# FFN of a four-layer decoder step: four plain tiles instead of three ahead of the paired ones, the input sums spread over two of them, the first down weights split ahead of the last gated value, adaLN loads spaced

## The reference

```
s1, a1, g1, s2, a2, g2 = split(silu(c) @ ada_w[i] + ada_b[i])
x <- LN(ALPHA * x + g1 * mixer(x * (1 + a1) + s1))
h  = x * (1 + a2) + s2
x <- LN(ALPHA * x + g2 * ((silu(h @ wg) * (h @ wu)) @ wd))      # wg, wu: 1024 x 2816, wd: 2816 x 1024
```

## Time and profile before

| | |
|---|---|
| median of 3 runs | 3110.5 us (3109.71 to 3116.89) |
| profiled execution | 3103.62 us, its span 3101.8 us |
| TensorE busy | 2932.5 us, 95% of the span |
| VectorE, ScalarE, GpSimd busy | 53%, 30%, 56% |
| mean granted TensorE clock | 0.98 of full speed |

### The profile page before, as it was taken

How to read it: one execution, slowest core, us unless ns; L and a number is a source line. 1 busy time by engine, 2 the same in 40 slices (tenths; PEclk the granted TensorE clock), 3 DMA queues, 4 the chain that set the end, 5 groups by cost and what they waited for, 6 DMA issues and landing times.

```text
span 3101.8 us, 53473 instructions
## 1 busy us (share of the span) xinstructions
PE 2932.5 (95%) x21172; PEld 2700.2 (87%) x21172; DVE 1653.5 (53%) x3161; ACT 934.4 (30%) x1825; POOL 1734.0 (56%) x1209
## 2 busy tenths in 40 slices
PE   6999989999999989999989998999999999899997
PEld 4799989999976879999986687999997999899997
DVE  3254684636554774635565547463553536846263
ACT  2220152414220442414234324241422211424141
POOL 2455456857666456767620154676764565468575
PEclk8999999999999999999999999999999999999999
DMA  6643333443345433444321433344422323222332
GB/s 239 224 116 86 119 114 98 136 130 102 99 122 159 151 120 97 162 126 160 94 64 56 115 122 104 109 151 130 157 74 83 102 85 93 62 82 82 87 92 72
DMA packets 450486, 354.85 MB, mean 114 GB/s; under 512 B 26120, under 2 KB 424832, under 8 KB 437933
## 3 DMA queue, kind: packets, MB, share of 16 engines
q1 hardware_dynamic: 435744, 324.79, 34.0%
q10 hardware_dynamic: 14493, 26.63, 2.9%
HBM read 337.86 MB, written 5.25 MB: 111 GB/s over the span
## 4 chain that ended last, share of the span: by engine, by line
PE 76%; DVE 10%; ACT 4%; DMA 2%; issue 2%; DVEq 2%; POOL 1%; ACTq 1%; POOLq 1%; SPq 1%
PE pb L1142 75%; DMA w_raw<-in_ffn_w_up 2%; DMA ada_first<-in_ada_w 1%; DVE part L2727 1%; ACT h_hi L2134 1%; ACT hf L2134 1%; DVE h_lo L2787 1%; DVE xa L2753 1%; DVE pb L2746 1%; DVE hf L2768 0%; DVE h_lo L2777 0%; PE pb L1978 0%; DVE a_lo L2594 0%; POOL a_lo L1048 0%; DVE part L2722 0%
## 5 line engine op out<-in xcount | busy, mean ns | idle before, releaser
L978 POOL TENSOR_SCALAR w_hi<-w_raw 128x1024 fp32r<-128x1024 f32 (+2 forms) x264 | 277.9, 1053 | 714.5 <-DMA w_raw<-in_gmlp_w_in 279.3
L981 POOL TENSOR_TENSOR w_lo<-w_raw,w_hi 128x1024 fp32r<-128x1024 f32 (+2 forms) x264 | 625.8, 2370 | 44.0 <-issue 44.0
L1142 PE MATMUL pb<-a_hi,w_hi 128*128 128x288 f32 x2176 | 601.7, 300 | 33.9 <-POOL w_hi L978 31.9
L1142 PE MATMUL pb<-a_lo,w_hi 128*128 128x288 f32 x2176 | 595.6, 297 | 0.0
L1142 PE MATMUL pb<-h_hi,w_hi 128*128 128x288 f32 x2064 | 548.7, 302 | 47.0 <-DVE pr L2939 19.4
L1142 PE MATMUL pb<-h_lo,w_hi 128*128 128x288 f32 x2064 | 528.7, 297 | 0.0
L1023 POOL TENSOR_TENSOR w_lo<-w_raw,w_hi 128x512 fp32r<-128x512 f32 x304 | 400.8, 1340 | 163.7 <-DVE s_raw L2979 106.6
L1142 PEld LDWEIGHTS pb<-a_hi,w_hi 128*128 128x128 f32 x2176 | 414.2, 190 | 42.1 <-issue 35.5
L1142 PEld LDWEIGHTS pb<-h_hi,w_hi 128*128 128x128 f32 x2064 | 382.8, 191 | 62.3 <-DVE pr L2939 20.4
L1142 PEld LDWEIGHTS pb<-a_lo,w_hi 128*128 128x128 f32 x2176 | 414.7, 191 | 0.7
L1142 PEld LDWEIGHTS pb<-h_lo,w_hi 128*128 128x128 f32 x2064 | 378.7, 191 | 0.0
(11 more groups left out here) (373 smaller groups left out, 4950.5 us busy)
## 6 DMA issues: line engine op xcount, KB each, us to landing
ada_w<-in_ada_w SPq DMA_DIRECT2D x80, 1024.0 KB, 8.9
w_raw<-in_ffn_w_gate SPq DMA_DIRECT2D x88, 512.0 KB, 3.9
w_raw<-in_ffn_w_up SPq DMA_DIRECT2D x88, 512.0 KB, 3.9
w_raw<-in_gmlp_w_in SPq DMA_DIRECT2D x64, 512.0 KB, 4.2
w_raw<-in_ffn_w_down SPq DMA_DIRECT2D x64, 512.0 KB, 5.0
w_raw<-in_gmlp_w_out SPq DMA_DIRECT2D x32, 512.0 KB, 4.9
w_raw<-in_ffn_w_down SPq DMA_DIRECT2D x32, 384.0 KB, 3.7
w_raw<-in_conv_w_pw SPq DMA_DIRECT2D x24, 512.0 KB, 4.2
```

What stands on the lines that cost most here:

```text
L978: nc.gpsimd.tensor_scalar(w_hi[:, s, 0:w], w_raw[:, s, 0:w], 1.0, 1.0, ALU.mult, ALU.mult).then_inc(split_hi, 1)
L981: nc.gpsimd.tensor_tensor(w_lo[:, s, 0:w], w_raw[:, s, 0:w], w_hi[:, s, 0:w].bitcast(F32), ALU.subtract).then_inc(split_lo, 1)
L1142: return nc.tensor.matmul(out, lhsT, rhs, start=start, stop=stop)
```

## The change

- Tile 3 of each layer becomes plain (`PAIRED_FROM = 4`), so four plain tiles run ahead of the first paired one, and two paired tiles are left in group 0.
- VectorE makes `t1`, then the two gated values of tiles 0 and 1, and only then `t3` and the changed `h`; the gated values of the plain tiles are formed in the bank of the up product (`gated_in_bank`): the product frees the gate's bank, and the `a_lo` subtraction the other. ScalarE's and GpSimd's orders follow: GpSimd makes `t4` ahead of the first pair's forms.
- At the end of a group the slots are taken in another order (`sums_end`): the slots of the tile before the last come first, then slot 4, then those of the last tile. GpSimd splits the first two down units ahead of the last tile's `gated_lower`.
- adaLN loads are asked for by `ada_asked`, one to four at a time, and two at a time ahead of the fifth and the seventh down unit of groups 0 and 1.

```diff
@@ -53,7 +53,8 @@
-PAIRED_FROM = 3
+GU = ((0, 6), (6, 8), (14, 8))
+PAIRED_FROM = 4
 QK = KT // 2
@@ -80,6 +81,18 @@
+def ada_asked(l, m):
+    if m <= 2:
+        return ADA1
+    done = [t for t in ada_groups(l)[0] if t <= m - 2]
+    if not done:
+        return ADA_FIRST + (0, 1, 2, 4)[min(m, 5) - 2]
+    last = max(done)
+    apart = any(last < first <= m for first, _ in GU)
+    return ada_used_by(l, m - 2) + (ADA1 if apart else min(ADA1, m - last))
@@ -523,7 +536,6 @@
-        GU = ((0, 6), (6, 8), (14, 8))
@@ -537,7 +549,8 @@
                 self.slot, self.prior, self.ordinal = [], [], []
-                self.held, self.last, self.whole = [None] * SLOTS, SLOTS - 1, 0
+                self.held, self.whole = [None] * SLOTS, 0
+                self.order, self.at, self.pairs = list(range(SLOTS)), 0, []
                 self.sums_free = {}
@@ -545,10 +558,12 @@
                 self.freed.append(None)
-                s = (self.last + 1) % SLOTS
-                if paired and s == SLOTS - 1:
-                    s = 0
-                self.last = s
+                if paired and self.order[self.at % SLOTS] == SLOTS - 1:
+                    self.at += 1
+                s = self.order[self.at % SLOTS]
+                self.at += 1
+                if paired:
+                    self.pairs = (self.pairs + [s])[-4:]
                 self.slot.append(s)
@@ -563,6 +578,7 @@
                 self.held[SLOTS - 1] = ("after", (acc_ready, self.products))
+                self.order, self.at = self.pairs[:2] + [SLOTS - 1] + self.pairs[2:], 0
@@ -692,7 +708,7 @@
                     plan.mark[l, "m", m] = len(plan.srcs)
-                    if m == 2:
+                    if m == PAIRED_FROM - 1:
                         plan.mark[l, "turned"] = plan.products - 2
@@ -859,8 +875,12 @@
                             load_to(plan.mark[l, "m", m])
-                            ada_to(l + 1, ADA1 if m < 4 else ada_used_by(l + 1, m - 3) + ADA1)
+                            ada_to(l + 1, ada_asked(l + 1, m))
                         if n < 2:
+                            load_to(plan.mark[l, "d", n] - 4)
+                            ada_to(l + 1, ada_used_by(l + 1, m) + 2)
+                            load_to(plan.mark[l, "d", n] - 2)
+                            ada_to(l + 1, ada_used_by(l + 1, m) + ADA1)
                             load_to(plan.mark[l, "d", n])
@@ -1067,14 +1087,13 @@
                         lower(t3_lo[:], t3_raw[:], t3_hi[:], t_low)
-                    forms_early(l, ms[0], FQ.n)
-                    if n == 0:
-                        pool.wait_ge(t_sum, 2 * l + 2)
+                        pool.wait_ge(t_sum, 3 * l + 3)
                         nc.gpsimd.tensor_tensor(t4_raw[:], h_hi[:, QK:, half_cols(0)].bitcast(F32), hf[:, 1],
                         pool.drain().then_inc(t4_made, 1)
+                    forms_early(l, ms[0], FQ.n)
                     for m in ms:
@@ -1083,8 +1102,9 @@
                             forms_early(l, m + 1, FQ.n)
+                    U.up(2 * len(ms))
+                    split_to(U.n + 2)
                     gated_lower(ms[-1] - GU[n][0])
-                    U.up(2 * len(ms))
@@ -1605,10 +1625,11 @@
                     first_halves(wait_h, 1, slots)
-                    s_a, s_b = take_units(2)
-                    for h in (1, 0):
-                        for s in (s_a, s_b):
-                            half_product(s, KT, h, (h_hi, h_lo))
+                    for _ in range(2, PAIRED_FROM):
+                        s_a, s_b = take_units(2)
+                        for h in (1, 0):
+                            for s in (s_a, s_b):
+                                half_product(s, KT, h, (h_hi, h_lo))
                 for m in paired_tiles(n):
@@ -2245,21 +2266,28 @@
                 if n == 0:
-                    for dst, src, at_ in ((t1_hi, t1_raw, 1), (t3_hi, t3_raw, 1)):
-                        act.wait_ge(t_sum, 2 * l + at_)
-                        fn(dst[:], src[:], ACT.Copy).then_inc(t_hi, 1)
                     first_gates()
-                    residuals(t, 0, 5)
+                    act.wait_ge(t_sum, 3 * l + 1)
+                    fn(t1_hi[:], t1_raw[:], ACT.Copy).then_inc(t_hi, 1)
+                    residuals(t, 0, 3)
+                    act.wait_ge(t_sum, 3 * l + 2)
+                    fn(t3_hi[:], t3_raw[:], ACT.Copy).then_inc(t_hi, 1)
                     gate(0, G.n % BANKS, ACT.Silu)
-                upper_gate(l, ms[0])
+                    residuals(t, 3, 6)
+                    gate(1, G.n % BANKS, ACT.Silu)
+                    upper_gate(l, ms[0])
+                    residuals(t, 6, 9)
+                    gate(0, G.n % BANKS, ACT.Silu)
+                    act.wait_ge(t_sum, 3 * l + 3)
+                    act.wait_ge(acc_ready, plan.mark[l, "turned"])
+                    fn(h_hi[:, 0:QK, half_cols(1)], hf[:, 1], ACT.Copy).then_inc(t_hi, 1)
+                else:
+                    upper_gate(l, ms[0])
                 upper_up(l, ms[0])
                 if n == 0:
-                    act.wait_ge(t_sum, 2 * l + 2)
-                    act.wait_ge(acc_ready, plan.mark[l, "turned"])
-                    fn(h_hi[:, 0:QK, half_cols(1)], hf[:, 1], ACT.Copy).then_inc(t_hi, 1)
+                    residuals(t, 9, 12)
                     gate(1, G.n % BANKS, ACT.Silu)
-                    residuals(t, 5, 10)
                 for m in ms:
@@ -2273,7 +2301,7 @@
                     if n == 0:
-                        residuals(t, 10 + 2 * (m - ms[0]), 11 + 2 * (m - ms[0]))
+                        residuals(t, 12 + 2 * (m - ms[0]), 13 + 2 * (m - ms[0]))
                     if m != ms[-1]:
@@ -2282,7 +2310,7 @@
                     if n == 0:
-                        residuals(t, 11 + 2 * (m - ms[0]), 12 + 2 * (m - ms[0]))
+                        residuals(t, 13 + 2 * (m - ms[0]), 14 + 2 * (m - ms[0]))
                     G.up(7)
@@ -2950,6 +2978,23 @@
+            def gated_in_bank(m, h, q):
+                up = pb[:, (G.n + 1) % BANKS, 0:HALF]
+                dve.wait_ge(acc_ready, G.n + 2)
+                dve.wait_ge(sg_ready, SG.up())
+                v.tensor_tensor(up, up, sg[:, q, :], ALU.mult).then_inc(acc_free, 1)
+                dve.drain()
+                v.tensor_copy(one(a_hi, m, half_cols(h)), up)
+                dve.drain()
+                v.tensor_tensor(one(a_lo, m, half_cols(h)), up, one(a_hi, m, half_cols(h)).bitcast(F32),
+                                ALU.subtract)
+                dve.drain().then_inc(a_ready, 1)
+                dve.sem_inc(acc_free, 1)
+                G.up(2)
@@ -3051,22 +3096,25 @@
                     v.tensor_tensor(t1_raw[:], t1_raw[:], h_lo[:, 0:QK, half_cols(0)].bitcast(F32), ALU.subtract)
+                    dve.drain().then_inc(t_sum, 1)
+                    for m in range(2):
+                        gated_in_bank(m, 1, m)
                     v.tensor_tensor(t3_raw[:], hf[:, 1], hf[:, 0], ALU.subtract)
                     ada_pairs(l + 1, ADA_FIRST * more)
-                    for m in range(2):
-                        gated(m, 1, m)
+                    gated_in_bank(2, 1, 0)
                     dve.wait_ge(t_hi, 4 * l + 1)
                     v.tensor_tensor(t1_lo[:], t1_raw[:], t1_hi[:].bitcast(F32), ALU.subtract).then_inc(t_lo_dve, 1)
+                    gated_in_bank(2, 0, 1)
                     form_sums(l, ms[0], FQ.n)
-                    gated(2, 1, 0)
+                    gated_in_bank(3, 1, 0)
                     dve.wait_ge(t_hi, 4 * l + 3)
                     form_lows(l, FQ.n)
-                    gated(2, 0, 1)
+                    gated_in_bank(3, 0, 1)
                 for m in ms:
```

## The result

The changed kernel takes 3022.4 us in the median (3020.06 to 3023.16, four runs) against 3110.5: 0.9711 of the time before, 95% interval 0.9694 to 0.9728, 88 us less. The forecast was 3025. The profiled execution takes 3020.06 us, its span 3018.3, which is 83.5 us less than before.

The account below looks back on a forecast made before the run. With TensorE at 95% of the span, gains come only where it idles or runs at its low clock. Starts 35.8, ends 41.7 and loads 7.8 sum to 85 us, from 3110.5 to 3025 us, range 3004 to 3070.

Parts of the forecast that it names:

- The starts: Four FFN starts: 41.0 us idle plus 16 of clock, less 14.8 of waits and 6.4 of added work, gains 35.8 us.
- left-over waits: TensorE's waits remaining at the FFN starts after the change: 3.7 us a layer, 14.8 in all.
- The three that the prediction names: Waits per start: first gated value 1.1 us, `w_lo` of tile 2's up 1.5, sum beside `t4_lo` 1.1.
- to 448.3: Layer 0's start: GpSimd's splits of tile 3's weights end at 448.3, wanted from 448.7; tile 3's 12.8 us cover later work.
- Rival 2: FFN starts gain nothing: GpSimd's two more splits make it last to be ready; 3067 us, chance 0.11.
- the clock: FFN starts: granted clock below 1 puts the windows 19 us short of full speed, of which 16 us taken as gain.
- The wait beside `t4_lo`: FFN starts: the sum for the next pair runs beside GpSimd's `t4_lo`; 0.7 to 1.5 us, taken as 1.1.
- The ends: Nine group ends, before the down products: 32.7 us idle plus 14 of clock, less 5 left over, gains 41.7 us.
- Rival 3: Ends gain nothing: a down unit lands late, GpSimd stands on it, TensorE waits in the second pass; 3067 us, chance 0.08.
- The loads: Inside the groups, adaLN loads delaying an up weight: 8.1 us idle plus 1.7 of clock, less 2 left, gains 7.8 us.
- rival 5: Slower: adaLN loads ahead of the fifth down unit make it land late, 120 us in all; 3145 us, chance 0.05.
- Rival 1: Short waits at the starts still drop the clock: 12 times 1.7, 20 us lost; 3045 us, chance 0.10.

Follow-up runs that it names:

- run 10: Changed kernel with the `w_hi` of tile 3's two weights cast by ScalarE in place of GpSimd: 3012.6 us, 0.9698.
- run 9: Changed kernel with four reorderings on VectorE, ScalarE and GpSimd, one for each wait left at the FFN starts: 3015.1 us, 0.9704.
- run 6: Changed kernel with `t3` and the fourth input sum again ahead of the first two gated values on VectorE, four plain tiles kept: 3024.2 us, 0.973.
- run 4: Changed kernel with the old slot rotation and the down weights' split behind the last `a_lo`, both end parts undone: 3069.5 us, 0.9879.
- Run 3: Changed kernel with the old rotation of slots at the group ends, the early split of the down weights kept: 3040.1 us, 0.9777.
- second trace: The changed kernel itself, measured again beside run 10 and 11: 3017.1 us, 0.9718.
- 11: The kernel of run 10 with three of the four reorderings of run 9, GpSimd's order as in the changed kernel: 3013.0 us, 0.9698.

## Why the prediction was right, and where its terms were not

**The starts** were forecast at 35.8 us and give 24.4 (253.6 to 229.2). Two sizes were off. The left-over waits were taken at 3.7 us a layer, 14.8; they are 21.4. The three that the prediction names come to 16.0 (5.6, 3.3 and 7.1); the other 5.4 are waits on the first pair's `w_lo` and on the kept p6, which it put at nothing. The step that failed is the sentence that tile 3's 12.8 us cover what stands behind it, the splits being done "to 448.3". They end at 451.75, in a trace that runs 1.2 us later: 2.3 us late. The prediction priced the collision of VectorE and GpSimd where `t3` meets the first split, and once more at `t4_lo`; it happens at nearly each large SBUF operation between (3.34, 2.69, 3.05 and 3.21 us on VectorE; 3.36, 2.16, 2.15 and 3.15 on GpSimd). In layer 0 the kept p6 hangs on GpSimd too, by way of ScalarE, which waits for the first pair's third form; VectorE then waits for ScalarE's next results:

```profile
462.74 0.63 ACT L2250 ACTIVATE w_hi<-w_raw 128x512 fp32r<-128x512 f32 x1 [1.91 <-POOLq L1053]
```

With two casts off GpSimd these two kinds of wait go (run 10), but for one of 0.4 us. That GpSimd's work alone sets the idle time of the starts is not shown: run 9 takes a third of it away by order alone, with GpSimd's work as long as before, and run 6 has all of it though GpSimd there stands idle for two gaps of 1.6 to 3.7 us in each layer. Rival 2 was thus right in a part of its mechanism and wrong in its size: GpSimd's added splits do make TensorE wait, for 6.6 us more than forecast in all left-over waits, not 35.8.

The other size is the clock, taken at 16 us; by difference it is 24.4 - 41.0 + 21.4 + 6.4 = 11.2. In the windows of the earlier trace rows TensorE is busy at the low clock for 32.1 us, and the forecast's 16 is half of that. Matmuls start 0.24 us apart there against 0.133 at full clock, so the low clock costs 0.45 of that time, 14.3 us. Layer 0 keeps 1.6 us of it after the change (its matmuls take 54.1 us, those of layer 2, as many, 52.5). The last 1.5 us stay open.

What was right: the first gated value (forecast wait 1.1, measured 1.25 to 1.6), the `w_lo` of tile 2's up (1.5; 1.1 in three layers, none in one), the 6.4 us of the extra tile, and the waits on `h_lo` gone. The wait beside `t4_lo` was there as foretold, 1.8 us in place of 1.1.

**The ends** were forecast at 41.7 us, with 5 left over; nothing is left over (179.90 of 180), so 46.7 by the same reckoning, and 50 by run 4. The steps hold as written: the splits end at 627.65, 2.6 us after the last product (forecast 2), the last `a_lo` come 2 us later and nobody waits for them. Run 3 shows how much cover there is: they may end 7.5 us after the first down product begins. Rival 3 falls.

**The loads** were forecast at 7.8 us; undone alone they cost 12. The old asking costs more beside the new starts (11.4 us of waits) than it did before (8.1). TensorE never waits for a down unit, so rival 5, the loads ahead of the fifth, falls.

The terms are 24.4, 50 and 12, together 86; the medians differ by 88, the forecast said 85. It was near because a term too large by 11 met two too small by 8 and 4 (these two by medians, good to some 6): that the sum fits to 3 us is luck. By kind of time the forecast did better: TensorE's idle time falls from 169.3 to 108.0 us, 61.3 against the 60 that its terms add up to, and its busy time from 2932.5 to 2910.3, so 28.6 us of clock with the 6.4 of added work, against 31.7.

**Rival 1**, that short waits drop the clock: of 19 waits of 0.4 to 1.8 us at the starts, one was followed by low clock (that of 1.78 us in layer 0; the window at 432 with 0.97), which costs 1.6 us, not 20. In the second trace it is again one, in layer 2. Four waits of 3.7 to 4.6 us in run 6 left the windows at 0.93 to 0.96.

## What to carry to other kernels

Where a helper engine is busy nearly without a break, list its rows from its first to its last before you price single waits, and price a collision of two engines at every pair of rows that overlap, not only where you first see it. A wait that is removed can come back at the next result that is wanted: by the stretch, less work for GpSimd gave 9 us here, reordering alone 2 and 8, both together 13, and each of the first three was expected at more. And a result that is right in sum says little about its terms; undo each part alone, and where the medians are too coarse, measure one stretch between two fixed instructions in the traces.

## What the hardware showed that I had not expected

VectorE and GpSimd hold each other up in whole instructions. The form sum out of SBUF (L3015) takes 0.70 us alone and 3.05 or 2.78 beside GpSimd, ending just after GpSimd's row; `w_hi` takes GpSimd 1.05 or 2.16. Of the 72 such form sums in the changed kernel's trace, 63 begin while a GpSimd row runs, and each of these ends 0.55 to 0.60 us after that row. The second form sum, with one operand in a bank, takes 0.70 at 455.02 though GpSimd works. The Trainium skill (GPSIMD Engine Reference, section Key points) says that GpSimd shares its SBUF interfaces with VectorE and that they contend where a VectorE instruction has two SBUF inputs or runs in a 2-port mode; the rows agree, and add the size.

The same wait does not cost the same low clock. Outside the FFN all kernels wait 5.4 us for the same product. Windows of TensorE there, in the changed kernel and then in run 10:

```profile
1549.00:1551.00 2.00, 0.00 (x0) 1.00 0.00 0
1551.00:1553.00 2.00, 0.49 (x3) 0.67 0.49 63
...
1557.00:1559.00 2.00, 1.43 (x7) 0.62 0.99 223
1559.00:1561.00 2.00, 1.60 (x13) 1.00 0.79 261
```

```profile
1544.00:1546.00 2.00, 0.00 (x0) 0.78 0.00 0
1546.00:1548.00 2.00, 0.59 (x3) 0.50 0.53 106
...
1556.00:1558.00 2.00, 2.00 (x11) 0.50 0.48 103
1558.00:1560.00 2.00, 2.00 (x16) 0.81 0.01 2
```

The clock is at its lower level (0.50, 1.2 GHz) for about 7 us in the one and 14 in the other, with the same work behind the wait. The Trainium skill (TensorE: Matmul & The Clock Gate, section What's actually happening) says that the monitor's windows run free of the kernel; that fits. Of the 14 traces, six have the short spell of low clock there and eight the long one, before and after both the short. A few such places a trace may be where runs 10 and 11 lost what their starts gained: the mean granted clock is 0.989 to 0.991 in their five timings each, and 0.991 to 0.993 in those of the changed kernel beside them. Which places these are, and why, stays open.
